# Compression's first product with its inputs stationary, in four column quadrants, and a selecting product behind it

## The reference, cut to what matters

```python
def _compress(tok, pos_emb, w1, w2):
    B, S, hd = tok.shape
    n_cmp = (S - CMP_LEN) // CMP_STRIDE + 1
    idx = np.arange(n_cmp)[:, None] * CMP_STRIDE + np.arange(CMP_LEN)[None, :]
    blocks = tok[:, idx] + pos_emb
    hid = jax.nn.gelu(blocks.reshape(B, n_cmp, CMP_LEN * hd) @ w1)
    return hid @ w2
...
    kc = _compress(k_cmp, cmp_pos_k, cmp_w1_k, cmp_w2_k)
    vc = _compress(v_cmp, cmp_pos_v, cmp_w1_v, cmp_w2_v)
```

## Time and profile before

| what | value |
|---|---|
| executions | 751.66, 752.17 and 754.02 us |
| median | 752.17 us |
| span of the profiled execution | 750.7 us, 15016 instructions |
| PE busy | 742.7 us (99%), 6374 matmuls |
| DVE busy | 601.2 us (80%) |
| ACT busy | 376.9 us (50%) |
| POOL busy | 30.6 us (4%) |
| DMA | 156.07 MB, mean 208 GB/s |

### The profile page before, as it was taken

How to read it: one execution, slowest core, us unless ns; L and a number is a source line. 1 busy time by engine, 2 the same in 40 slices (tenths; PEclk the granted TensorE clock), 3 DMA queues, 4 the chain that set the end, 5 groups by cost and what they waited for, 6 DMA issues and landing times.

```text
span 750.7 us, 15016 instructions
## 1 busy us (share of the span) xinstructions
PE 742.7 (99%) x6374; PEld 733.2 (98%) x6374; DVE 601.2 (80%) x897; ACT 376.9 (50%) x506; POOL 30.6 (4%) x22
## 2 busy tenths in 40 slices
PE   8999999999999999999999999999999999999998
PEld 8999999999999999999999999999999999999997
DVE  5756889889897788998998788979787886687554
ACT  6558255745676533443434547356556553434330
POOL 0000000004000000000000000201110000000000
PEclk9999999999999999999999999999999999999999
DMA  9844373342843459999987336655344565678511
GB/s 336 319 153 146 110 275 113 113 139 108 309 174 115 169 173 389 334 349 329 335 306 271 138 127 230 224 174 219 103 173 139 205 224 173 224 281 301 201 58 56
DMA packets 24113, 156.07 MB, mean 208 GB/s; under 512 B 3568, under 2 KB 3696, under 8 KB 6000
## 3 DMA queue, kind: packets, MB, share of 16 engines
q1 hardware_dynamic: 24048, 155.13, 57.6%
HBM read 154.07 MB, written 1.05 MB: 207 GB/s over the span
## 4 chain that ended last, share of the span: by engine, by line
PE 95%; DVE 2%; ACT 1%; DMA 1%; issue 1%; DVEq 0%; SPq 0%
PE bank L786 17%; PE bank L787 16%; PE bank L788 16%; PE bank L867 9%; PE bank L870 9%; PE bank L869 9%; PE bank L794 3%; PE bank L796 3%; PE bank L797 3%; PE bank L1272 2%; PE bank L1239 1%; PE bank L1249 1%; PE bank L1169 1%; DMA sb_raw<-in_stream 1%; PE bank L1322 0%
## 5 line engine op out<-in xcount | busy, mean ns | idle before, releaser
L1742 DVE TENSOR_TENSOR sb_lo<-sb_raw,sb_hi 128x2048 fp32r<-128x2048 f32 (+1 forms) x116 | 261.7, 2259 | 74.5 <-ACT sb_hi L1406 74.1
L1406 ACT CAST sb_hi<-sb_raw 128x2048 fp32r<-128x2048 f32 (+1 forms) x116 | 217.8, 1882 | 100.7 <-PE bank L870 49.3
L786 PE MATMUL bank<-sb_u_hi,sb_hi 128*128 128x256 f32 (+2 forms) x696 | 195.4, 281 | 0.0
L787 PE MATMUL bank<-sb_u_lo,sb_hi 128*128 128x256 f32 (+2 forms) x696 | 192.7, 277 | 0.0
L788 PE MATMUL bank<-sb_u_hi,sb_lo 128*128 128x256 f32 (+2 forms) x696 | 192.6, 277 | 0.0
L786 PEld LDWEIGHTS bank<-sb_u_hi,sb_hi 128*128 128x128 f32 (+2 forms) x696 | 129.6, 186 | 3.0 <-issue 2.2
L787 PEld LDWEIGHTS bank<-sb_u_lo,sb_hi 128*128 128x128 f32 (+2 forms) x696 | 129.8, 186 | 0.3
L788 PEld LDWEIGHTS bank<-sb_u_hi,sb_lo 128*128 128x128 f32 (+2 forms) x696 | 129.7, 186 | 0.2
L867 PE MATMUL bank<-sb_hid_hi,sb_hi 128*128 128x256 f32 x432 | 119.3, 276 | 0.0
L870 PE MATMUL bank<-sb_hid_hi,sb_lo 128*128 128x256 f32 x432 | 119.2, 276 | 0.0
L869 PE MATMUL bank<-sb_hid_lo,sb_hi 128*128 128x256 f32 x432 | 119.2, 276 | 0.0
(11 more groups left out here) (368 smaller groups left out, 1330.3 us busy)
## 6 DMA issues: line engine op xcount, KB each, us to landing
sb_raw<-in_stream SPq DMA_DIRECT2D x140, 1024.0 KB, 5.2
sb_raw<-in_stream SPq DMA_DIRECT2D x4, 256.0 KB, 6.6
sb_raw<-in_stream SPq DMA_DIRECT2D x2, 512.0 KB, 8.5
sb_mem_t<-in_mem SPq DMA_DIRECT2D x1, 1024.0 KB, 4.8
out<-sb_h SPq DMA_DIRECT2D x4, 256.0 KB, 2.2
sb_const<-in_constants SPq DMA_DIRECT2D x1, 830.0 KB, 10.8
sb_h<-in_x SPq DMA_DIRECT2D x1, 572.0 KB, 3.6
sb_h<-in_x SPq DMA_DIRECT2D x1, 512.0 KB, 7.0
```

Source lines behind the costliest of these rows:

```text
L786: nc.tensor.matmul(out, a_hi, b_hi, start=(i == 0), stop=False)
L787: nc.tensor.matmul(out, a_hi, b_lo, start=False, stop=False)
L1406: nc.scalar.copy(place(hi, s)[:, 0:n], x[:, 0:n]).then_inc(sem("hi_ready"), 1)
L1742: tt(place(lo, s)[:, 0:n], x[:, 0:n], f32(place(hi, s)[:, 0:n]), ALU.subtract) \
```

## The change

It touches only the compression's first product. In the new `cmp_product(i)` the operands change places: 32 columns of cmp_in (the slices k and its neighbour) are stationary and the 128 columns of a weight slice stream. The results of slice k go to partitions 32 (k mod 4) and the 31 behind them, so the bank holds four partial sums of 32 rows, each with 16 rows that belong to even slices and 16 that belong to odd ones, of which half are wanted. All 16 slices are multiplied in one call ahead of the gate block. ACT copies the 128x128 result into the first 256 columns of prob_t (`cmp_product` on ACT, a new step). A new step `cmp_sum(i)` on PE, between the halves of the gate block, multiplies this copy by a new constant pick (128x16, which selects and adds the wanted rows) and so gives the same 16 columns as before. The rest of `cmp_hidden` is unchanged.

ACT has a new step in its list, at the place of `cmp_product`. SP's wait for the slot of the compression's weights now goes by the new product's bank. The constants are 16 columns wider, and an unused tile is 16 columns narrower.

```diff
-                if step[0] == "cmp_product" and step[2] == 0:
+                if step[0] == "cmp_product":
                     raw.append(("cmp_w1", step[1]))
...
-    steps([("cmp_product", 0, 0)])
-    block("gate", 3, between=[("cmp_product", 0, 1), ("cmp_hidden", 0), ("topk", 0, 0)])
-    steps([("cmp_product", 1, 0), ("topk", 0, 1), ("turn_qk", 2)])
-    block("gate", 4, between=[("cmp_product", 1, 1), ("cmp_hidden", 1), ("cmp_hid",), ("topk", 0, 2)])
+    steps([("cmp_product", 0)])
+    block("gate", 3, between=[("cmp_sum", 0), ("cmp_hidden", 0), ("topk", 0, 0)])
+    steps([("cmp_product", 1), ("topk", 0, 1), ("turn_qk", 2)])
+    block("gate", 4, between=[("cmp_sum", 1), ("cmp_hidden", 1), ("cmp_hid",), ("topk", 0, 2)])
...
+    put("pick", (i % 32 - 16 * (i // 32 % 2)) == np.arange(16)[None, :])
...
+        cmp_parts = prob_t[:, 0, 0:256].rearrange("p (i n) -> p i n", i=2)
...
-            def cmp_product(i, part):
+            def cmp_product(i):
 
-                key = ("cmp_hidden", i)
+                key = ("cmp_parts", i)
                 w = shaped(raw_ready(pe, ("cmp_w1", i)), ("cmp_w1", i))
-                ps = banks[lease[key][0]] if part else claim(key, "turn")
+                ps = claim(key, "turn")
                 pe.wait_ge(sem("cmp_in_ready"), i + 1)
-                x = cmp_in[:, i, :].rearrange("p (k n) -> p k n", k=16)
-                for k in half(16, part):
-                    last = nc.tensor.matmul(ps[:, 0:16], w[:, k, :], x[:, k, :], start=(k == 0), stop=(k == 15))
-                if part:
-                    fill(last, key)
+                for k in range(16):
+                    r = slice(32 * (k % 4), 32 * (k % 4) + 32)
+                    pair = 16 * (k - k % 2)
+                    last = nc.tensor.matmul(ps[r, 0:P], cmp_in[:, i, pair:pair + 32], w[:, k, :], start=(k < 4),
+                                            stop=(k >= 12), skip_group_check=True)
+                fill(last, key)
+
+            def cmp_sum(i):
+
+                wait_evacuated(pe, ("cmp_parts", i))
+                ps = claim(("cmp_hidden", i), "turn")
+                fill(nc.tensor.matmul(ps[:, 0:16], cmp_parts[:, i, :], cst("pick"), start=True, stop=True),
+                     ("cmp_hidden", i))
...
+            def cmp_product(i):
+
+                key = ("cmp_parts", i)
+                ps = wait_filled(act, key)
+                free(nc.scalar.copy(cmp_parts[:, i, :], ps[:, 0:P]), key)
...
-                        wait_filled(sp, ("cmp_hidden", before[1]))
+                        wait_filled(sp, ("cmp_parts", before[1]))
```

More of the change, by code:

```diff
@@ L59 @@
 CONST_WIDTHS = dict(ident=P, suffix=P, prefix=P, ones=P, causal=2 * P, strict=3 * P, cos1=64, sin1=64, nsin1=64,
-                    cos2=128, sin2=128, nsin2=128, cmpneg=2 * NC, cmp01=2 * NC, decay=RH * 2 * P)
+                    cos2=128, sin2=128, nsin2=128, cmpneg=2 * NC, cmp01=2 * NC, pick=16, decay=RH * 2 * P)
 CONST_AT = dict(zip(CONST_WIDTHS, np.cumsum([0] + list(CONST_WIDTHS.values())).tolist()))
@@ L583, in two_blocks_kernel @@
         rden = sb(ctx, "rden", [P, 24, 2])
-        sb(ctx, "gap", [P, P // 4])
+        sb(ctx, "gap", [P, P // 4 - 16])
         turned_hi = sb(ctx, "turned_hi", [P, 2, T], F32R)
@@ L1370, in _ @@
             run(dict(block=take, mem_v=mem_v, raw=raw_product, ssq_cols=ssq_cols, rstd_row=rstd_row, turn_qk=turn_qk, turn_tail=turn_tail, stick=stick, suffix=suffix,
-                     pv_stick=pv_stick, index=index, turn_cmp=turn_cmp, cmp_product=cmp_product, cmp_kv=cmp_kv,
+                     pv_stick=pv_stick, index=index, turn_cmp=turn_cmp, cmp_product=cmp_product, cmp_sum=cmp_sum, cmp_kv=cmp_kv,
                      cmp_scores=cmp_scores, turn_cmp_p=turn_cmp_p, cmp_pv=cmp_pv, scores=scores, turn_p=turn_p,
@@ L1660, in _ @@
                  "turn_qk": turn_qk, "turn_tail": turn_tail, "stick": stick, "suffix": suffix, "gates_c": gates_c,
-                 "cmp_hidden": cmp_hidden,
+                 "cmp_product": cmp_product, "cmp_hidden": cmp_hidden,
                  "cmp_kv": cmp_kv, "cmp_scores": cmp_scores, "turn_cmp_p": turn_cmp_p, "scores": scores,
```

## The result

| what | before | after |
|---|---|---|
| median of the executions | 752.45 us (4) | 758.49 us (4: 757.23, 758.40, 758.58, 759.15) |
| span of the profiled execution | 750.7 us | 755.3 us |
| PE busy | 742.7 us | 742.1 us |
| DVE busy | 601.2 us | 602.3 us |

The ratio is 1.0074 (95% interval 1.0060 to 1.0089): 6.0 us slower, where 2.85 had been forecast and the range ended at 758.0. The direction and the stall came out as written, the size did not, and one loss was not in the forecast at all.

A forecast was written before the change was run, and what follows sets the result against it. Around 100 us DVE's list, fed by PE, was taken to set the time, so PE's saved 4.3 us go into a stall; 752.17 plus 1.45 (delay) plus 1.4 (clock) gave 755.0 us, range 752.8 to 758.0.

The forecast's parts named there:

- The product and the sum: New work on PE: 1.25 us per four-quadrant product, 0.22 per selecting sum; 2.9 us in all instead of 7.2.
- the other end: Upper price of one new product on PE, its 32 passes running one after another: 3.4 plus 0.40, 3.8 us.
- The copy's place and the stall: ACT copies behind gate 2's tanh, 93.60 to 93.86, so PE stands 5.2 us at the keys' cmp_sum.
- What the stall costs at the second copy: DVE's copy at 100.74 moves to 102.19; both engines leave that stretch 1.45 us later.
- The clock: PE's clock drops in the stall, so work behind it runs at half speed: bounds 0 and 1.8, taken 1.4 us.
- The discount for executions that lose less: Clock loss set at 1.4, under the start's 1.8 us, as not every execution need lose all.
- The way to the end: DVE's chain carries the delay to 119.11, where PE waits; behind that PE is the chain, so it reaches the end.
- The clock stays up: Rival: PE's clock holds through the 5.2 us stall; only +1.45, 753.6 us; chance 0.27.
- Quadrants one after another: Rival: the new product's quadrants don't overlap, 3.8 us each; +4.0, 756.2 us, up to 757.6 with clock fall; chance 0.17.
- The gain arrives: Rival: PE doesn't wait for gate 2's tanh, 4.3 us come off: 747.9, more likely 751.8; chance 0.04.

The follow-up runs named there:

- e4: Kernel after with ACT's copy ahead of gate 2's evacuation (gate 3's likewise) and all 32 passes in one quadrant (result not the compression): 755.35 us, ratio 1.0037.
- e2: Kernel after with 21 dummy products keeping PE busy in the stall ahead of the keys' sum: 755.39 us, ratio 1.0045.
- e12: Kernel after with 21 dummy products in PE's stall and GpSimd's second addition held until DVE's residue is done: 755.89 us, ratio 1.0035.
- e11: Kernel after, unchanged, measured again in another batch beside other executions of the kernel before: 757.34 us, ratio 1.0056.
- e5: Kernel after with GpSimd's second addition made to wait until DVE is through with the residue: 757.16 us, ratio 1.0063.
- e8: Kernel before with five dummy products on PE (1.11 us) ahead of the values' product: 753.51 us, ratio 1.0018.
- e1: Kernel after with ACT's copy step moved ahead of gate 2's evacuation, and likewise gate 3's: 753.67 us, ratio 1.0018.
- e7: Kernel before with the ten copies of turn_cmp made by ACT instead of DVE: 752.23 us, ratio 1.0002.
- e6: Kernel after with ACT's copy ahead of gate 2's and gate 3's evacuations and turn_cmp's ten copies on ACT instead of DVE: 751.62 us, ratio 0.9999.
- e3: Kernel after with 10 dummy products in PE's stall ahead of the keys' sum, PE still idle 2.91 us: 757.38 us, ratio 1.0067.

## Why the prediction was wrong in size and right in kind

**The product and the sum, right.** 1.25 us was taken for the product in four quadrants, it took 1.0; the other end, 3.8, was measured in e4 as 3.7. 0.22 was taken for the sum; at full clock it takes 0.13 from its first pass to the next block's (104.07 to 104.20).

**The copy's place and the stall, right.** ACT's copy was forecast for 93.60 to 93.86 and ran from 93.67 to 93.92. The stall was to be 5.2 us and was 4.97. DVE's first copy was to be at 94.5 and was at 94.61.

**What the stall costs at the second copy, a little too high.** +1.45 was worked out. With the clock held up it was +1.15 (e2) and +1.14 (e12). Most of the difference is the product, 0.25 us shorter than assumed.

**The clock, the mis-sized term.** It was bounded by 0 and 1.8 us and set at 1.4, from the start of the kernel. Its measured size is 2.5 us in the half block alone (5.40 less 2.91), and 2.5 and 2.2 at the copy (after and e11, less e2 and e12). The failing step is the upper bound. The start was taken as the most that a cold stretch can cost: 17 passes of 256 columns at the slow spacing. Behind the stall the whole half block of 24 passes ran at it in after. In e11 and e5 the spacing fell back before its end (at 99.25 and 98.50 us), and their copies are 3.33 and 2.95 us late instead of 3.66. The bound that the rows allowed was the half block at the start's spacing, 24 x 0.21 = 5.0 us instead of 2.9, and more if the product followed at that level. The discount for executions that lose less went the wrong way too: all eight have the same mean clock, 0.995, and the least loss in a profile of after or e5 is 2.95 - 1.15 = 1.8 us, the bound itself. The rule of the Trainium skill that the prediction weighed here ("TensorE: Matmul & The Clock Gate", "HAM oscillation — how this bites in real kernels": waits between bursts bring the lower clock back) holds in this kernel: 0.50 behind the stall, 1.00 with the stall filled.

**The way to the end, a missed term.** "Behind that PE is the chain, so it reaches the end" holds for a delay alone (e8). In after another 1.0 us came at the merge, where the chain goes over DVE a second time. The row for that was in the trace: PE starts the out block after 0.18 us of idle time at 183.26, and the residue before it began 0.13 us ahead of GpSimd's addition. The prediction followed the chain to 119 us and did not look for the next such place. It could have priced the risk, 1.05 us if the order turns, but not foreseen the turn, which hangs on 0.20 us in the spacing of PE's passes.

**The sum, made again.** 0.06 ahead of the change, 1.15 for the stall, 2.5 for the clock, 0.99 at the merge, -0.1 behind it: 4.6 us, the difference of the two spans, where the prediction had 1.45 and 1.4 and nothing for the merge. With the median it is 6.0 in one measurement and 4.2 in the other.

**The rivals.** "The clock stays up" is what e2 made: 755.39 instead of the 753.6 given to it, since the microsecond at the merge was missing there too and another came behind it, which has no name (568.45 us from the merge to the end instead of 567.44). "Quadrants one after another" is what e4 priced, with the copy first. "The gain arrives" is what e1 made possible. The prediction gave that case 751.8 if DVE has no more than 0.40 us to spare. DVE was that full (0.35 us earlier at its copy), and the time came to 753.67, with the merge and a fall of the clock behind e1's own waits on top. The reason given, that DVE was busy back to back, is not quite so: 0.83 us of waiting for ACT lie in between the earlier trace rows, and no run tried to shorten them.

**What stays open.** Between the merge and the end the spans of the other kernels scatter from 567.1 to 568.5 us (span less merge in the table; e12 569.3). Runs of PE's passes are spaced 0.113 us in some blocks and 0.118 in others, and which block has which differs between the profiled executions. What decides it was not tried, and by it the order of GpSimd and DVE is open as well. Nor is it known why the same kernel after stood at +6.0 us in one measurement and at +4.2 in the other, nor why the profiled execution of after took 758.40 us, 3.1 more than its span, where the three others took 1.8 to 1.9 more.

## What to carry to other kernels

When an edit adds a step to an engine that walks a list in order, first ask what stands ahead of it there and whom that waits for. The copy cost 0.25 us, its place some 5 us of PE. A saving on an engine that feeds a full one is worth only what the full one can be relieved by: at DVE's second copy the change with its copy in the right place gave 0.35 us (e1), the relief alone nothing (e7), both together 2.44 (e6). And a delay has to be followed to the end through every handover, not only the first one, and counted from an instruction ahead of the change, since the executions here differed by up to 1 us before they came to it.

## What the runs showed of the hardware

- **Column quadrants in float32.** 32 passes of 128 columns on 32 stationary columns: 1.08 us in four quadrants, 3.68 us in one.
- **The clock falls behind short waits.** Behind 2.91 us of PE's idle time the next half block ran at a granted clock of 0.50 (e3). Behind 5 us of it the passes of 256 columns were 0.21 us apart up to 98.4 us in e5, 99.1 in e11 and 99.5 in after, each counted on its own profile, and 0.11 to 0.12 after that. In e1 two waits of 1.11 and 0.91 us, whose ends are 1.6 us apart, were followed by a stretch at 0.54; in e6 waits of 0.51 and 0.85 us, 8.7 us apart, by none. The prediction had no row for either.
- **DVE and GpSimd on SBUF.** An addition of 1.29 us on GpSimd and a subtraction of 2.29 us on DVE, begun 0.07 to 0.13 us apart, took 3.36 us for the second to begin, whichever engine that was. A shift of 0.2 us between the two decides a whole microsecond at the next handover to PE.
- **Two spacings of the same passes.** Passes of 256 columns at the full granted clock are 0.113 us apart in some blocks and 0.118 in others, and one block has either in different profiles (0.118 in after, 0.113 in e3, ahead of the split near 180 us).
